# Seven block products instead of eight for a feed-forward layer's gate and up projections, in float32 split into high and low parts

## The chip, the cores and the metric

The kernel runs on one core of a Trainium2 chip. The metric is the device time of one execution in microseconds (us). The core's engines are TensorE (PE, the matrix multiplier; PEld are its weight loads), VectorE (DVE), ScalarE (ACT), GpSimd (POOL) and SyncE (SP, which here only issues DMA transfers). They run their own instruction streams and wait for each other through semaphores. TensorE writes its results to PSUM (8 banks of 128 x 512 float32); everything else lies in SBUF.

## The reference

Two transformer blocks in a row, 1024 tokens of width 1024. Both end in the same kind of feed-forward layer, and the change is to it:

```python
h = rms_norm(h_res, pre_ffn_g[l])                                    # 1024 x 1024
f = silu(einsum('bld,df->blf', h, w_gate[l])) * einsum('bld,df->blf', h, w_up[l])   # d_ff = 2816
f = einsum('blf,fd->bld', f, w_down[l])
h_res = h_res + rms_norm(f, post_ffn_g[l])
```

The second block has the same with `w_ffn_in` (gate and up side by side) and `w_ffn_out`. Before the layer stands the mixer's output projection (`w_out`), a norm and a residual; what the mixers compute (differential attention with a state space model, gating with forgetting attention) plays no part here.

## The kernel before

All matrices are float32. Each operand of a product is split into a high part, rounded to the format that TensorE takes at full rate (float32r), and a low part, the rest. A product is then three matmuls into one PSUM bank, in the helper `three` (L267 to L271): high x high, high x low, low x high.

The input of the layer, transposed (features on partitions), is `xh` and `xl`: 8 feature tiles of 128 x 1024 tokens. D_FF = 2816 makes NF = 22 inner tiles of 128.

Class `Mlp` (L1656) does the layer, for both blocks:

- `pe_in` computes gate (j = 0, banks 0 and 1) or up (j = 1, banks 2 and 3) of one inner tile: 8 feature tiles x 2 token halves x 3 = 48 matmuls of 128x512. `pe_hidden` is both, 96 matmuls.
- ScalarE (`act_hidden`) takes SiLU of the gate from PSUM into `f`, VectorE (`dve_prod`, L1847) multiplies it with up from PSUM, ScalarE makes the high part `mlp_fh` (L1832), VectorE the low part `mlp_fl` (`dve_low`, L1852).
- `pe_down` multiplies a pair of inner tiles with their rows of the down weights: 8 token tiles x 2 column halves x 2 inner tiles x 3 = 96 matmuls, into banks 4, 5 and 6, 7 by turns. VectorE adds each token tile's result to `hbuf` (`dve_add`, L1858, 128x1024), which a memset cleared.
- In the loop of `pe` the order is hidden(f+2), down of the pair before, hidden(f+3); one trip of the loop holds three such pairs (864 matmuls) and there are three trips. Each engine has its own loop.
- The weights come as 512 KB loads on SP's queue into `mlp_raw` (one buffer each for gate, up and down); GpSimd makes both parts (`pool_split`: high L1716, low L1719), each some 128x1024 operation.

Around it: `pe_out` does the output projection. Beside its second half run, tile by tile, `act_beside_out`, `dve_beside_out`, `pool_beside_out` and `sp_beside_out`: square sums (ScalarE, L488), roots (GpSimd, `pool_root1` and `pool_root2`, L500 and L504), norm, residual and scaling (VectorE, L515, L521, L527, the last into `xs_b`), transposition on TensorE (`pe_turn`, L546), high part (ScalarE, L495) and low part (VectorE, L535) of `xh`, `xl`. Before the roots `pool_beside_out` splits the first two weight tiles. `pe_first` is the entry of the layer: it puts the first inner tile's gate and up, by token halves, between the turns of tiles 4 to 7. The last pair of down products (`pe_down_tile` with NP-1) stands alone at the end.

## Time and profile before

| | us |
|---|---|
| runs, median of 3 | 2792.04 (2789.49 to 2795.03) |
| the profiled execution | 2792.63 |
| its span, first to last instruction | 2790.8 |
| TensorE busy in the span | 2565.2 (92%) |
| VectorE, ScalarE, GpSimd busy | 1060.0, 531.4, 915.0 |
| mean granted TensorE clock | 0.958 of full speed |

Busy times of matmuls overlap in the profile, since they are pipelined, so the distance between the starts of matmuls says what one costs. The chain of waits is followed back from the last instruction to what released each; it says which engine's work sets the end. In the lists of single instructions the columns are start, duration, engine, line, operation, output <- inputs, shape and count, and in brackets the engine's idle time before it and who ended it. "issue" is a wait for which the profile shows no other releaser.

### The profile page before, as it was taken

To read this page: it belongs to the slowest core of one execution; us is meant where nothing else is said; L and a number is where in the kernel's file an instruction comes from. 1 tells how busy PE (TensorE), PEld (TensorE's weight loads), DVE (VectorE), ACT (ScalarE), POOL (GpSimd) and SP (SyncE) were. 2 spreads that over 40 slices of the span, in tenths; PEclk is the share of its full clock that TensorE was granted. 3 is DMA by queue.
4 is the path that set the end of the run, shared out by engine and by line. 5 is a ranking of instruction groups with operands and counts; after the bars stand their busy time and mean duration, and the time that the engine had idled before them with its cause. 6 is when DMAs were issued, how large, how long until landed. Compare 5 with 4: busy or idle time off the path is not lost.

```text
span 2790.8 us, 30673 instructions
## 1 busy us (share of the span) xinstructions
PE 2565.2 (92%) x12294; PEld 2073.0 (74%) x12294; DVE 1060.0 (38%) x1624; ACT 531.4 (19%) x1008; POOL 915.0 (33%) x571
## 2 busy tenths in 40 slices
PE   8998777489999999999989998877999999999997
PEld 8977655377788888888878886765778878878885
DVE  5984655436322222222264313663432222222224
ACT  4221344414100000000032002442310000000001
POOL 3210300015433333344374432000553333333332
PEclk8998899689999999999999999996999999999998
DMA  4437300004111111111142112000411111111113
GB/s 134 132 118 195 124 15 1 4 31 159 61 46 46 46 46 46 46 46 46 49 162 64 51 47 91 1 9 16 151 61 46 46 46 46 46 46 46 46 46 128
DMA packets 175980, 180.20 MB, mean 65 GB/s; under 512 B 38344, under 2 KB 138568, under 8 KB 175840
## 3 DMA queue, kind: packets, MB, share of 16 engines
q1 hardware_dynamic: 169968, 163.95, 19.0%
q10 hardware_dynamic: 5872, 14.22, 1.5%
q8 instruction: 107, 1.75, 0.2%
q14 instruction: 33, 0.27, 0.0%
HBM read 147.65 MB, written 30.49 MB: 64 GB/s over the span
## 4 chain that ended last, share of the span: by engine, by line
PE 83%; DVE 6%; ACT 4%; issue 2%; DMA 2%; POOL 2%; SPq 0%; ACTq 0%; POOLq 0%; DVEq 0%
PE ps L269 23%; PE ps L271 23%; PE ps L270 23%; PE ps L1497 3%; PE ps L1527 3%; PE ps L1513 2%; ACT ex L1574 2%; DMA msb<-ssm_lags 1%; DVE hbuf L515 1%; DVE hbuf L521 1%; PE ps L546 1%; DVE hbuf L1858 1%; PE ps L1502 1%; PE ps L2289 1%; PE ps L2242 0%
## 5 line engine op out<-in xcount | busy, mean ns | idle before, releaser
L1847 DVE TENSOR_TENSOR mlp_f<-mlp_f,ps 128x1024 f32<-128x1024 f32 x44 | 53.7, 1221 | 831.6 <-PE ps L271 802.0
L1716 POOL TENSOR_TENSOR mlp_w2h<-mlp_raw,ones 128x1024 fp32r<-128x1024 f32 x44 | 83.4, 1895 | 817.7 <-PE ps L271 732.4
L209 POOL TENSOR_TENSOR wgt<-raw,ones 128x512 fp32r<-128x512 f32 x76 | 86.9, 1143 | 770.5 <-PE ps L271 615.5
L1858 DVE TENSOR_TENSOR hbuf<-hbuf,ps 128x1024 f32<-128x1024 f32 x176 | 214.8, 1220 | 243.6 <-PE ps L271 243.6
L269 PE MATMUL ps<-mlp_w2h,mlp_fh 128*128 128x512 f32 x704 | 280.4, 398 | 11.4 <-issue 7.4
L269 PE MATMUL ps<-xh,mlp_w0h 128*128 128x512 f32 x704 | 278.5, 396 | 7.4 <-ACT mlp_f L1828 5.1
L269 PE MATMUL ps<-xh,mlp_w1h 128*128 128x512 f32 x704 | 278.9, 396 | 2.8 <-DVE xl L535 2.8
L270 PE MATMUL ps<-mlp_w2l,mlp_fh 128*128 128x512 f32 x704 | 279.3, 397 | 0.0
L271 PE MATMUL ps<-mlp_w2h,mlp_fl 128*128 128x512 f32 x704 | 279.3, 397 | 0.0
L270 PE MATMUL ps<-xl,mlp_w1h 128*128 128x512 f32 x704 | 278.7, 396 | 0.0
L271 PE MATMUL ps<-xh,mlp_w1l 128*128 128x512 f32 x704 | 278.7, 396 | 0.0
L271 PE MATMUL ps<-xh,mlp_w0l 128*128 128x512 f32 x704 | 278.0, 395 | 0.0
L270 PE MATMUL ps<-xl,mlp_w0h 128*128 128x512 f32 x704 | 278.0, 395 | 0.0
L1828 ACT ACTIVATE mlp_f<-ps 128x1024 f32<-128x1024 f32 x44 | 45.2, 1027 | 785.6 <-PE ps L271 785.6
L269 PEld LDWEIGHTS ps<-mlp_w2h,mlp_fh 128*128 128x128 f32 x704 | 133.3, 189 | 46.4 <-issue 8.2
L269 PEld LDWEIGHTS ps<-xh,mlp_w0h 128*128 128x128 f32 x704 | 132.3, 188 | 41.1 <-issue 9.5
L269 PEld LDWEIGHTS ps<-xh,mlp_w1h 128*128 128x128 f32 x704 | 132.7, 188 | 35.0 <-DVE xl L535 3.3
L271 PEld LDWEIGHTS ps<-mlp_w2h,mlp_fl 128*128 128x128 f32 x704 | 133.1, 189 | 32.1
L270 PEld LDWEIGHTS ps<-mlp_w2l,mlp_fh 128*128 128x128 f32 x704 | 133.2, 189 | 31.7
L271 PEld LDWEIGHTS ps<-xh,mlp_w1l 128*128 128x128 f32 x704 | 132.7, 188 | 32.0
L270 PEld LDWEIGHTS ps<-xl,mlp_w1h 128*128 128x128 f32 x704 | 132.6, 188 | 31.8
L271 PEld LDWEIGHTS ps<-xh,mlp_w0l 128*128 128x128 f32 x704 | 132.3, 188 | 31.8
(389 smaller groups left out, 4783.0 us busy)
## 6 DMA issues: line engine op xcount, KB each, us to landing
mlp_raw<-in_w_ffn_in SPq DMA_DIRECT2D x44, 512.0 KB, 4.3
h<-hbuf SPq DMA_DIRECT2D x24, 512.0 KB, 2.8
mlp_raw<-in_w_gate SPq DMA_DIRECT2D x22, 512.0 KB, 4.5
mlp_raw<-in_w_up SPq DMA_DIRECT2D x22, 512.0 KB, 4.9
mlp_raw<-in_w_down SPq DMA_DIRECT2D x22, 512.0 KB, 4.6
mlp_raw<-in_w_ffn_out SPq DMA_DIRECT2D x22, 512.0 KB, 4.1
raw<-in_w_in SPq DMA_DIRECT2D x40, 256.0 KB, 2.6
raw<-in_w_out SPq DMA_DIRECT2D x32, 256.0 KB, 2.7
```

The lines of the kernel that those rows point to most:

```text
L209: nc.gpsimd.tensor_tensor(wh[:, s, :], r, ones[:, 0:1].broadcast_to([P, 512]), ALU.mult).then_inc(w_hi, 1)
L269: pe.matmul(out, lhs[0], rhs[0], start=first, stop=False)
L270: pe.matmul(out, lhs[0], rhs[1], start=False, stop=False)
L271: return pe.matmul(out, lhs[1], rhs[0], start=False, stop=last)
L1497: pe.matmul(self.score(item, m, a, b), self.q[rows, t, i * P:(i + 1) * P], self.k[rows, t, a:b], start=True, stop=True)
L1513: t = pe.transpose(ps[0:w, self.tbank(b), j * P:(j + 1) * P], self.ex[:, n % 3, 0, c:c + w], ident[:, :])
L1527: mm = pe.matmul(self.obank(n), self.atb[0:w, b % 3, j, :], self.v[0:w, t, h * self.dv:(h + 1) * self.dv], start=first, stop=last, skip_gr ...
L1574: nc.scalar.activation(self.ex[:, n % 3, m, 0:w], src, ACT.Exp, bias=negmax[:, n % 3, m:m + 1], accum_out=psum_l[:, n % 3, m:m + 1]).then_ ...
L1716: nc.gpsimd.tensor_tensor(self.sh[j][:, b, :], self.raw[:, j, :], ones[:, 0:1].broadcast_to([P, D]), ALU.mult).then_inc(self.s[f"hi{j}"], 1)
L1828: nc.scalar.activation(self.f[:, :], ps[:, 0:2, :].rearrange("p b c -> p (b c)"), ACT.Silu)\
L1847: v.tensor_tensor(self.f[:, :], self.f[:, :], ps[:, 2:4, :].rearrange("p b c -> p (b c)"), ALU.mult).then_inc(self.s["prod"], 1)
L1858: v.tensor_tensor(self.acc[:, i, :], self.acc[:, i, :], ps[:, b:b + 2, :].rearrange("p b c -> p (b c)"), ALU.add)\
```

## The change

Gate and up of one inner tile are seen as one product of a 2 x 2 block matrix (gate and up; low and high half of the 1024 features) with the 2 x 2 blocks of the input (feature halves x token halves). Strassen's algorithm, in the form with 7 products and 15 additions, is used. With gl, gh, ul, uh for the weight blocks (128 x 512) and b11, b21, b12, b22 for those of x:

- weights: s1 = ul + uh, s2 = s1 - gl, s3 = gl - ul, s4 = gh - s2 (GpSimd, `pool_sum`, per inner tile, in float32 before the split)
- input: t1 = b12 - b11, t2 = b22 - t1, t4 = b21 - t2, t3 = b22 - b12, once per layer, built on TensorE by adding matmuls with the identity `posid` or its negative `negid` onto the turned tile in PSUM (`add_block`, `pe_t24`, `pe_t3`: 40 matmuls of 128x512), with high part by ScalarE (`act_t`) and low part by VectorE (`dve_t`); t1 takes the place of b12 in `xh`, `xl`
- products, 12 matmuls each: gl b11, gh b21 (added in bank X), s1 t1 and s4 b22 (bank Z), s2 t2, s3 t3, uh t4 (bank Y, one after the other on top)
- VectorE adds the partial results out of PSUM as they come (u2, u3, p1, half-width 128x512), with SiLU by ScalarE on the two gate halves

The down products are done per inner tile: 48 matmuls, each result added by VectorE, in four pairs of token tiles between the block products; only the last two inner tiles are taken together (96 matmuls). The first result is copied, not added, so the memset goes. ScalarE takes over all high parts (`act_hi`), GpSimd does sums and low parts in half-width operations (low part over the raw weights). The loops have 9 trips of two windows (264 matmuls). The new order of TensorE in a window (one inner tile):

```diff
+        def pe_window(self, pe, f, odd, down=True, begun=False):
+            x = self.BX[odd]
+            early = isinstance(f, int) and f < 2
+            def down_pair(n):
+                if down:
+                    self.pe_down_tile(pe, f - 1, 2 * n)
+                    self.pe_down_tile(pe, f - 1, 2 * n + 1)
+            if not begun:
+                if not early:
+                    self.wait(pe, "prod", f * 2 - 2)
+                self.pe_product(pe, f, odd, "gl", x, True)
+                self.wait(pe, "taken", f * 5 - 1)
+            self.pe_product(pe, f, odd, "s1", self.BZ, True)
+            down_pair(0)
+            if begun:
+                begun()
+            else:
+                self.wait(pe, "taken", f * 5)
+            self.pe_product(pe, f, odd, "s2", self.BY, True)
+            down_pair(1)
+            self.wait(pe, "taken", f * 5 + 1)
+            self.pe_product(pe, f, odd, "s3", self.BY, False)
+            down_pair(2)
+            if not begun:
+                self.pe_x_second(pe, f, odd)      # gh
+            down_pair(3)
+            self.wait(pe, "taken", f * 5 + 3)
+            self.pe_product(pe, f, odd, "s4", self.BZ, False)
+            self.pe_product(pe, f, odd, "uh", self.BY, False)
```

GpSimd, ScalarE and VectorE in the same window (g is the next inner tile, whose weights are prepared):

```diff
+        def pool_window(self, pool, f, odd):
+            g, o = f + 1, 1 - odd
+            self.pool_sum(pool, g, o, "s1", f * 5 + 1)
+            self.pool_lo(pool, g, o, "uh")
+            self.pool_sum(pool, g, o, "s2", f * 5 + 2)
+            self.pool_lo(pool, g, o, "s1")
+            self.pool_sum(pool, g, o, "s3", f * 5 + 3)
+            self.pool_lo(pool, g, o, "gl")
+            self.pool_lo(pool, g, o, "s3")
+            self.pool_sum(pool, g, o, "s4", f * 5 + 4)
+            self.pool_lo(pool, g, o, "s2")
+            self.pool_down_lo(pool, f)
+            self.pool_lo(pool, g, o, "gh")
+            self.pool_lo(pool, g, o, "s4")
...
+        def act_window(self, act, f, odd, middle=None):
...
+                for name in ("uh", "s1", "gl", "s2", "s3"):
+                    self.act_hi(act, g, o, name)
+            self.wait(act, "direct", f * 2 + 2)
+            nc.scalar.activation(x, x, ACT.Silu).then_inc(self.s["x_read"], 1)
...
+                self.act_hi(act, g, o, "gh")
+            self.wait(act, "taken", f * 5 + 4)
+            nc.scalar.activation(self.u2[:, :], self.u2[:, :], ACT.Silu).then_inc(self.s["x_read"], 1)
+            self.act_f_hi(act, f, 1)
...
+                self.act_hi(act, g, o, "s4")
+            self.wait(act, "raw_down", (f + 1) * 16)
+            z = 0 if more else 1
+            nc.scalar.copy(self.d[z][0][:, :], self.d_raw[z][:, :]).then_inc(self.s["f_hi"], 1)
+            self.act_f_hi(act, f, 0)
...
+            adds(4, NT)
+            self.wait(v, "mixed", f * 5 + 4)
+            v.tensor_tensor(u2, u2, z, ALU.add).then_inc(taken, 1)
+            self.wait(v, "x_read", f * 3 + 3)
+            v.tensor_tensor(u3, u2, u3, ALU.mult).then_inc(self.s["prod"], 1)
+            self.wait(v, "mixed", f * 5 + 5)
+            v.tensor_tensor(p1, p1, y, ALU.add).then_inc(taken, 1)
+            self.wait(v, "taken", f * 5 + 5)
+            v.tensor_tensor(p1, p1, x, ALU.mult).then_inc(self.s["prod"], 1)
+            b = 0 if self.last(f) else 1
+            for h, src in ((1, u3), (0, p1)):
+                c = slice(h * HALF, (h + 1) * HALF)
+                self.wait(v, "f_hi", f * 3 + (1 if h else 3))
+                v.tensor_tensor(self.f[b][1][:, c], src, self.f[b][0][:, c].bitcast(F32), ALU.subtract)\
+                    .then_inc(self.s["f_lo"], 1)
```

SP loads the raw down weights of a window once the down tiles of the inner tile before are done, since they lie where the low part lay:

```diff
+            self.wait(sp, "down", f * 8)
+            sp.dma_start(self.d_raw[0][:, :], self.wd[:, bass.ds(f, 1), :].rearrange("p f n -> p (f n)"))\
+                .then_inc(self.s["raw_down"], 16)
```

The entry: turns of tiles 4 to 7 with the additions onto them, and products gl and gh of inner tile 0 between:

```diff
+            turns.pe_turn(pe, 4)
+            out_emptied(pe)
+            turns.x_ready(pe, 3)
+            self.pe_product(pe, 0, 0, "gl", self.BX[0], True)
+            turns.pe_t24(pe, 0)
+            turns.pe_turn(pe, 5)
+            turns.pe_t3(pe, 0)
+            self.pe_x_second(pe, 0, 0)
+            turns.pe_t24(pe, 1)
+            turns.pe_turn(pe, 6)
+            turns.pe_t3(pe, 1)
+            turns.pe_t24(pe, 2)
+            turns.t_ready(pe, 0, 3)
+            turns.pe_turn(pe, 7)
+            turns.pe_t3(pe, 2)
+            turns.pe_t24(pe, 3)
+            turns.t_ready(pe, 2, 3)
...
+            self.pe_window(pe, 0, 0, False, rest)
+            self.pe_window(pe, 1, 1)
+            with pe.Fori(0, 9) as it:
                 for b in range(2):
+                    self.pe_window(pe, it * 2 + (2 + b), b)
+            self.pe_window(pe, NF - 2, 0)
+            self.pe_window(pe, NF - 1, 1, False)
             for i in range(NT):
+                self.pe_down_tile(pe, NF - 2, i, both=True)
```

`pool_beside_out` no longer waits and splits two full weight tiles ahead of the roots: it makes s1 and the low part of uh, and the other blocks of inner tile 0 between the roots, one or two half-width operations at a time. The gains and the scaled tile get buffers of their own for each of the two passes, and the next gains are loaded inside the last window. The weight slots of the output projection and of the second block's projections are dealt in another order.

## Rows read from the trace of the kernel before

**Rows 1.** The page: shares of the chain that ended last.
```profile
PE 83%; DVE 6%; ACT 4%; issue 2%; DMA 2%; POOL 2%; SPq 0%; ACTq 0%; POOLq 0%; DVEq 0%
PE ps L269 23%; PE ps L271 23%; PE ps L270 23%; PE ps L1497 3%; PE ps L1527 3%; PE ps L1513 2%; ACT ex L1574 2%; DMA msb<-ssm_lags 1%; DVE hbuf L515 1%; DVE hbuf L521 1%; PE ps L546 1%; DVE hbuf L1858 1%; PE ps L1502 1%; PE ps L2289 1%; PE ps L2242 0%
```
**Rows 2.** Busy us by stretch: PE, PEld, DVE, ACT, POOL, clock, DMA share, GB/s.
```profile
1260.00:1340.00 80.00, 80.00 (x345) 64.35 (x344) 15.05 (x12) 5.19 (x5) 36.02 (x17) 1.00 0.19 60
```
**Rows 3.** Single matmuls in order of time, first feed-forward layer.
```profile
716.35 0.47 PE L269 MATMUL ps<-xh,mlp_w0h 128*128 128x512 f32 x1 [2.58 <-ACT mlp_f L1828]
...
1141.75 0.40 PE L271 MATMUL ps<-xh,mlp_w1l 128*128 128x512 f32 x1
```
**Rows 4.** Instructions in order of time, entries of both feed-forward layers.
```profile
644.65 0.22 POOL L500 TENSOR_SCALAR tmpa<-stat 128x1 f32<-128x1 f32 x1
...
654.40 1.97 PE L546 MATMUL ps<-ident,xs_b 128*128 128x128 f32 x8 [3.46 <-DVE xs_b L527]
...
682.71 0.40 PE L271 MATMUL ps<-wgt,gyl 128*128 128x512 f32 x1
...
1965.38 1.29 POOL L211 TENSOR_TENSOR wgt<-raw,wgt 128x512 fp32r<-128x512 f32 x1
...
1993.26 1.10 PE L546 MATMUL ps<-ident,xs_b 128*128 128x128 f32 x8 [1.43 <-DVE xs_b L527]
...
2018.90 0.40 PE L271 MATMUL ps<-wgt,mbl 128*128 128x512 f32 x1
...
2050.99 0.47 PE L269 MATMUL ps<-xh,mlp_w0h 128*128 128x512 f32 x1 [2.57 <-ACT mlp_f L1828]
```
**Rows 5.** Single matmuls, start of the last down products, first layer.
```profile
1414.96 0.77 PE L269 MATMUL ps<-mlp_w2h,mlp_fh 128*128 128x512 f32 x1 [3.70 <-issue]
1415.52 0.63 PE L270 MATMUL ps<-mlp_w2l,mlp_fh 128*128 128x512 f32 x1
```
**Rows 6.** Operations on two tiles: duration in ns min/median/max, first and last start.
```profile
L1847 DVE TENSOR_TENSOR mlp_f<-mlp_f,ps x44: 1220/1221/1224, 716.3 to 2747.2; 128x1024 f32<-128x1024 f32 x44
L1852 DVE TENSOR_TENSOR mlp_fl<-mlp_f,mlp_fh x44: 1218/1417/3461, 718.7 to 2749.5; 128x1024 fp32r<-128x1024 f32 x44
L1719 POOL TENSOR_TENSOR mlp_w0l<-mlp_raw,mlp_w0h x44: 2396/2407/3271, 637.8 to 2680.8; 128x1024 fp32r<-128x1024 f32 x44
```
**Rows 7.** Instructions in order of time, behind products of TensorE.
```profile
783.62 0.40 PE L269 MATMUL ps<-xh,mlp_w0h 128*128 128x512 f32 x1
783.82 1.22 DVE L1858 TENSOR_TENSOR hbuf<-hbuf,ps 128x1024 f32<-128x1024 f32 x1 [1.58 <-PE ps L271]
783.86 1.90 POOL L1716 TENSOR_TENSOR mlp_w2h<-mlp_raw,ones 128x1024 fp32r<-128x1024 f32 x1 [40.35 <-PE ps L271]
...
828.61 1.22 DVE L1847 TENSOR_TENSOR mlp_f<-mlp_f,ps 128x1024 f32<-128x1024 f32 x1 [18.28 <-PE ps L271]
829.87 1.05 ACT L1832 CAST mlp_fh<-mlp_f 128x1024 fp32r<-128x1024 f32 x1 [11.43 <-DVE mlp_f L1847]
```
**Rows 8.** Groups of instructions of half width: busy us, mean ns, idle before.
```profile
L535 DVE TENSOR_TENSOR xl<-ps,xh 128x512 fp32r<-128x512 f32 x48 | 30.8, 682 | 18.9 <-ACT xh L495 18.9
L495 ACT CAST xh<-ps 128x512 fp32r<-128x512 f32 x48 | 25.5, 584 | 33.0 <-PE ps L546 33.0
```
**Rows 9.** The weight loads: a wait of GpSimd, and landing times.
```profile
791.85 1.90 POOL L1716 TENSOR_TENSOR mlp_w2h<-mlp_raw,ones 128x1024 fp32r<-128x1024 f32 x1 [3.61 <-DMA mlp_raw<-in_w_down]
...
DMA to landing us min/median/max: 3.4/4.6/8.8
```
**Rows 10.** Single matmuls behind the four returns of TensorE's loops.
```profile
940.40 0.40 PE L269 MATMUL ps<-xh,mlp_w0h 128*128 128x512 f32 x1
...
1142.30 0.49 PE L269 MATMUL ps<-xh,mlp_w0h 128*128 128x512 f32 x1
...
2275.18 0.49 PE L269 MATMUL ps<-xh,mlp_w0h 128*128 128x512 f32 x1 [0.89 <-issue]
...
2478.28 0.50 PE L269 MATMUL ps<-xh,mlp_w0h 128*128 128x512 f32 x1 [1.26 <-issue]
```

More of the change, by code:

```diff
@@ L1891, in _program, with dve @@
+        def dve(self, v):
+            self.dve_window(v, 0, 0, False)
+            v.wait_ge(sem("stored"), 16 * NT * (1 + 2 * self.turn))
+            self.dve_window(v, 1, 1)
+            with v.Fori(0, 9) as it:
+                for b in range(2):
+                    self.dve_window(v, it * 2 + (2 + b), b)
+            self.dve_window(v, NF - 2, 0)
+            self.dve_window(v, NF - 1, 1, False)
+            self.wait(v, "f_lo", 2 * NF)
     o1 = at("o1", [P, NT, HALF], F32, O_X)
```

570 lines of the change are left out of this document (327 added, 243 removed).

## Prediction

> **What bounds the kernel now.** I read the page's totals and its chain of waits first, then the table of stages, then the feed-forward stages by groups, then single instructions where something waits. Both feed-forward blocks together take about half of the span, and TensorE is on 83% of the chain that ended last, and 69% of the span lies in the three lines of the helper `three` [rows 1]. In the middle of a feed-forward block TensorE is busy for 80.00 of 80 us at granted clock 1.00, while VectorE works 15 us of the 80 and GpSimd 36 [rows 2]. So a matmul less there is time less, as long as nobody new has to be waited for. The price of one: matmul 1 of `pe_hidden(1)` starts at 716.35, matmul 1824 (96 + 2 x 864) at 1141.75; that is 0.2333 us each, gate, up and down alike [rows 3]. Outside this steady part there are two places where TensorE waits: the entry (it waits for the first tile's `xs_b`, for the tiles' turns, and for SiLU's first result) and the end (3.70 us before the last down products, and then some matmuls that last 0.63 instead of 0.40 us, at the lower of the two clocks) [rows 4, 5].
>
> **What is removed.** Inner tiles 1 to 21 of each block take 7 x 12 = 84 gate/up matmuls instead of 96: 21 x 12 = 252 fewer. The down matmuls are as many as before (20 x 48 + 96 = 1056). 2 x 252 x 0.2333 = **-117.6 us**. The 8 more VectorE additions per pair of tiles (1.22 us each [rows 6]), and the smaller splits on GpSimd and ScalarE are in the shade of a window of 132 matmuls = 30.8 us: VectorE 8 x 1.22 + 9 x 0.68 = 15.9, GpSimd 11 x 1.3 + 2.4 = 16.7, ScalarE some 9 us. The memset that goes (one per block) was not on TensorE's path. SP issues five loads per inner tile (four of 256 KB, one of 512) for three of 512 KB; the bytes are the same, and each waits only for a product of the window before the one that needs it, down excepted (below). Neither engine becomes the bound by its sum; what matters is the order inside a window.
>
> **The one tight chain in a window.** Let 0 be the end of product s4 (so uh runs 0 to 2.8, the next window's gl to 5.6, s1 to 8.4, and at 8.4 down pair 0 wants this tile's `f` and `down` parts). A consumer starts 0.20 (VectorE) or 0.24 us (GpSimd) after the start of TensorE's next matmul, and ScalarE 0.04 us after VectorE's end (828.61 + 1.22 to 829.87) [rows 7]. Half-width operations (128x512) take 0.68 on VectorE, 0.59 on ScalarE [rows 8], 1.29 on GpSimd [rows 4]. At 0.20 VectorE adds z to u2 (to 0.9), ScalarE does SiLU (to 1.6), VectorE wants the product u3 at 1.6 to 1.7. GpSimd makes sum s4 from 0.24 to 1.53 and begins `lo s2` at 1.60. The product has both inputs in SBUF. Such a VectorE operation is what gets long when GpSimd works: `mlp_fl` (both inputs SBUF) takes 1.22 to 3.46 us, `mlp_f` (one input PSUM) 1.220 to 1.224 always, and GpSimd's 2.41 becomes 3.27 in turn [rows 6]. One waits for the whole instruction of the other. If GpSimd is first: product 2.9 to 3.5; ScalarE: f high half 2 to 4.1, high part of s4 to 4.7, high part of down (1.05) to 5.7, f half 1 to 6.2. The raw down weights are there by then: after `down` is done (-2.6), today's next load of the same 512 KB keeps GpSimd waiting for 3.61 us in all [rows 9], so about 1.0. GpSimd's low part of down runs 5.75 to 8.15; VectorE's low part of f half 1, ready at 6.3, must wait until 8.15 and ends at 8.8. TensorE begins pair 0 at 8.9 instead of 8.4, everything behind it in its queue (s2, s3, gh, s4, uh) moves with it, and with a slow first matmul, as behind other stops (0.1), that is **0.6 us in each of the windows 1 to 20: 40 x 0.6 = +24 us**. If VectorE is first at 1.6, everything is 1.1 us earlier and pair 0 has no wait. The two differ by 0.1 us in the order at 1.6, which I cannot settle from rows; I take GpSimd first, since its 1.60 needs two steps and VectorE's 1.65 needs three handovers. Bounds: 0 and 1.0 per window (eight handovers, each up to 0.05 longer than I took it), 0 to 40 us.
>
> The Trainium skill ("SBUF — State Buffer", Terms) says of the port pair that VectorE and GpSimd share that it is locked for the full instruction and that the loser fully blocks. The rows of `mlp_fl` agree (3.46 less 1.22 is nearly one GpSimd operation of 2.41). Without that rule, with shared bandwidth, the chain would be short enough for no stop.
>
> **The entry.** Today from the last out-projection matmul's end to `pe_hidden(1)`: (last start 682.71 or 2018.90, plus 0.23) 682.94 to 716.35 = 33.4 us, and 2019.13 to 2050.99 = 31.9 [rows 3, 4]. After: inner tile 0's products and 40 more matmuls (9.3 us) that build t2, t4, t3, each tile of them needing a ScalarE copy and a VectorE subtraction, in order, behind the turn. I walked it: turn 4 and its additions 0.9 to 2.2, gl to 5.0, wait for `lo` of tile 4 (6.4), pe_t24(0) to 8.0, turn 5 to 9.2. ScalarE: casts for tile 5 (2 x 0.53), square (1.2), keep, t2 to 12.4; VectorE to 13.1. Then t3(0), gh, pe_t24(1), turn 6 to 20.5. Each later tile repeats turn 1.3 + casts 1.1 + three T copies 1.6 + subtraction 0.7 + t3 0.5 + t24 1.4, about 6.5 us: turn 7 ends 26.8, s1 starts 32.1 and ends 34.9. Window 0 has no down pairs to cover VectorE: wait for t3's last tile 2.0, s2 2.8, wait 1.1, s3 2.8, wait 1.6, s4 and uh 5.6: 50.8. One stretch of lower clock after an idle of 4 us, as after the 3.70 us one [rows 5] (8 matmuls, each some 0.2 longer): 52.4. So 19.0 and 20.5 us longer than now. Against it: GpSimd no longer splits two full weight tiles (2 x (1.90 + 2.41) = 8.6 us [rows 6, 9]) ahead of the first root, which starts at 644.65 [rows 4], but does a half-width sum and a low part (2.6), with ScalarE's first square then the later of the two, so the first `xs_b` is some 5 us earlier; the waits of 3.46 us (with the lower clock behind it some 2.0 more, as in [rows 5]) and 1.43 us before `pe_turn(0)` go [rows 4]: -5.5 and -1.6. Entries together **+32.4 us**. Its bounds: +17, if the walk's 39.5 us are only 0.6 of that because the copies of T overlap better than in my order; +45, if TensorE's clock is low for most of the entry.
>
> **The end.** In window 21 there are no down pairs, so s3 waits 1.1 us for VectorE. Then the f parts lie over fz, so ScalarE does f half 2 (0.59) and the down part (1.05) only after uh, GpSimd 2.4: 4.4 us instead of 3.7. **+3.6 us** for both.
>
> **The loops.** TensorE returns to a loop's head 2 times per block now: 0.0, 0.4, 1.2, 1.5 us beyond the pitch (mean 0.8) [rows 3, 10]. After: 8 returns per block. They come between uh and gl, so they lie inside the 0.6 us stop where that exists: 16 x 0.25 - 3.1 = **+1 us**; without that stop 16 x 0.6 - 3.1 = +6.5. The Trainium skill ("Runtime: NRT & Kernel Launch", Instruction fetch mechanics) says that a taken branch outside the resident window forces a fetch before execution goes on, and gives 2048 instructions for TensorE. The present body (1728 matmul and load instructions plus waits) would hardly fit, the new one (528 plus waits) would, and then all returns would be free; the row with 0.0 shows that size alone does not force a stop.
>
> **Sum** against the profiled execution (2792.6 us, span 2790.8; its median of runs is 2792.0, so the same): 2792.6 - 117.6 + 24 + 32.4 + 3.6 + 1 = **2736 us**.
>
> **Rivals.**
> A (forecast, 0.5): GpSimd wins the port at s4's end; 2736.
> B (0.25): VectorE wins, no stop at pair 0: 2792.6 - 117.6 + 32.4 + 3.6 + 6.5 = 2717.5. For it: VectorE's three operations could hand over in 0.03 us each, as some do [rows 7].
> C (0.12): each return costs the 1.5 us of the longest row, on top of the stop: 2736 - 1 + 16 x 1.5 - 3.1 = 2756. Against it: the other returns are cheaper.
> D (0.06), slower: the raw down weights land late. They can be asked for only when down tile 7 is done, 11 us before they are needed as parts. At the longest landing of this kernel's weight loads, 8.8 us [rows 9], ScalarE starts its part at 6.3, GpSimd ends at 9.8, VectorE at 10.5, and pair 0 stops 2.2 us: 40 x 2.25 = 90, 2801 us. It decides from 2.0 us a window (81 / 40). Against it: the median is 4.6, and today the next load follows alone in its queue, as here.
> The rest (0.07) is other faster outcomes. A stop of 0.6 us does not cost the clock: after an idle time of 1.26 us [rows 10] and even 2.57 us [rows 4] the next matmul took 0.50 and 0.47 us, not 0.77 as behind the 3.70 us [rows 5].
>
> **Numbers.** Predicted 2736; range 2708 to 2772 (B and its entry a little better; C and a worse entry). About 0.2% is what a measurement of this kernel tells from no change. Faster 0.92 (A, B, C and the rest), same 0.02, slower 0.06 (D).
>
> **What would show it.** TensorE instructions lower by 2 x (252 + 12 - 40) = 448 matmuls. Pair 0's first matmul with an idle time of about 0.5 us put down to VectorE's low part of f (A) or none (B); the product u3 lasting 1.9 us rather than 0.7 (A). From the out-projection's end to the start of window 1 about 52 us. GpSimd's first root some 4 us earlier against the out-projection. The prediction is wrong if the pitch is not 0.233, if idle stands before a product other than those named, or if the T part takes much more or less than 20 us over today's.

## The result and the profile after

The changed kernel took 2704.61 us (median of 4 runs, 2693.33 to 2706.45), the kernel before 2790.76 beside it: ratio 0.9682, 95% interval 0.9652 to 0.9711, so 3.2% faster. The forecast was 2736 with a range from 2708 to 2772. The side was right; the time lies 31 us below the forecast and 3 us below the range. The profiled execution of after, 2693.33 us with a span of 2691.2, is the fastest of its four. The account by stages below compares spans (2790.8 before, a difference of 99.6 us); a second set of runs of the unaltered kernel gave 2697.65 us (2696.16 to 2704.77) and a span of 2694.6.

The shares of the chain that ended last, from the page of after, and the table of stages of after over the same 80 us as in [rows 2]:

```profile
PE 80%; DVE 7%; ACT 5%; issue 3%; DMA 2%; POOL 2%; SPq 0%; ACTq 0%; POOLq 0%; DVEq 0%
PE ps L267 22%; PE ps L268 22%; PE ps L269 22%; PE ps L1546 3%; PE ps L1576 3%; PE ps L1562 2%; ACT ex L1623 2%; DVE hbuf L513 1%; PE ps L562 1%; DMA msb<-ssm_lags 1%; DVE hbuf L2045 1%; PE ps L1551 1%; PE ps L2528 1%; PE ps L2480 1%; PE ps L436 1%
```
```profile
1260.00:1340.00 80.00, 80.00 (x349) 65.27 (x348) 46.65 (x46) 20.19 (x34) 44.51 (x31) 1.00 0.16 49
```

TensorE is busy for all of the 80 us at granted clock 1.00, as before, but with 349 matmuls instead of 345. So each is shorter, which the forecast had no term for. VectorE went from 15.05 to 46.65 us and GpSimd from 36.02 to 44.51; neither is the bound.

Single matmuls of after in order of time, first layer: the start of windows 1 and 21.

```profile
731.49 0.40 PE L267 MATMUL ps<-xh,mlp_glh 128*128 128x512 f32 x1
...
1339.36 0.40 PE L267 MATMUL ps<-xh,mlp_glh 128*128 128x512 f32 x1
```

(1339.36 - 731.49) / 20 = 30.39 us a window, 0.2302 us a matmul, against 0.2333 in [rows 3] and 30.8 us a window in the forecast. No window in between is longer, so there is no stop in them and no gap at the loop's returns.

The entry of the first layer, matmuls in order of time; the last out-projection matmul is the row at 679.17:

```profile
651.95 1.10 PE L544 MATMUL ps<-ident,xs_a 128*128 128x128 f32 x8 [0.94 <-DVE xs_a L525]
...
679.17 0.40 PE L269 MATMUL ps<-wgt,gyl 128*128 128x512 f32 x1
...
685.95 0.50 PE L562 MATMUL ps<-xh,negid 128*128 128x512 f32 x1 [1.81 <-DVE xl L533]
...
692.42 0.79 PE L562 MATMUL ps<-xh,negid 128*128 128x512 f32 x1 [3.46 <-DVE t2l L600]
...
702.87 0.80 PE L562 MATMUL ps<-xh,negid 128*128 128x512 f32 x1 [2.76 <-DVE t2l L600]
...
717.45 0.50 PE L267 MATMUL ps<-t2h,mlp_s2h 128*128 128x512 f32 x1 [1.40 <-DVE t3l L600]
...
721.27 0.50 PE L267 MATMUL ps<-t3h,mlp_s3h 128*128 128x512 f32 x1 [0.78 <-DVE mlp_u L2063]
...
725.82 0.50 PE L267 MATMUL ps<-xh,mlp_s4h 128*128 128x512 f32 x1 [1.50 <-DVE mlp_u L2068]
```

From 679.17 + 0.23 to 731.49 are 52.1 us (forecast 52.4; 33.4 before by [rows 3, 4]). In the second layer, 1967.93 + 0.23 to 2018.26, they are 50.1 (31.9 before). The waits stand where the forecast's walk had them: for the low part of the last split tile, for each tile's T copies, and in window 0 before s2, s3 and s4. The lower clock (matmuls of 0.63 us) came twice in the first entry, behind the waits of 3.46 and 2.76 us, where the walk had it once.

The end, in answer to [rows 5]:

```profile
1365.15 0.76 PE L267 MATMUL ps<-mlp_dh,mlp_fh 128*128 128x512 f32 x1 [5.12 <-POOL mlp_dzl L1846]
1365.71 0.63 PE L268 MATMUL ps<-mlp_dl,mlp_fh 128*128 128x512 f32 x1
```

5.12 us of idle time (4.89 in the second layer) instead of 3.70, and the same 0.63 us matmuls behind it.

The place on which the forecast turned, s4's end, in the middle of the first layer of after: instructions of VectorE, GpSimd and ScalarE in order of time, then pair 0's first matmul, which shows no idle time.

```profile
880.87 0.69 DVE L2071 TENSOR_TENSOR mlp_u<-mlp_u,ps 128x512 f32<-128x512 f32 x1 [1.50 <-PE ps L269]
880.91 1.30 POOL L1833 TENSOR_TENSOR mlp_s_raw<-mlp_gh_raw,mlp_s_raw 128x512 f32<-128x512 f32 x1 [7.08 <-PE ps L269]
881.59 0.63 ACT L2016 ACTIVATE mlp_u<-mlp_u 128x512 f32<-128x512 f32 x1 [2.83 <-DVE mlp_u L2071]
882.25 0.69 DVE L2073 TENSOR_TENSOR mlp_u<-mlp_u,mlp_u 128x512 f32<-128x512 f32 x1 [0.70 <-ACT mlp_u L2016]
882.29 1.81 POOL L1840 TENSOR_TENSOR mlp_s2l<-mlp_s_raw,mlp_s2h 128x512 fp32r<-128x512 f32 x1
...
885.22 2.71 POOL L1846 TENSOR_TENSOR mlp_dl<-mlp_d_raw,mlp_dh 128x1024 fp32r<-128x1024 f32 x1 [1.12 <-ACT mlp_dh L2022]
885.75 2.73 DVE L2082 TENSOR_TENSOR mlp_fl<-mlp_p,mlp_fh 128x512 fp32r<-128x512 f32 x1
...
889.01 0.39 PE L267 MATMUL ps<-mlp_dh,mlp_fh 128*128 128x512 f32 x1
```

The product u3 starts at 882.25 and GpSimd's low part of s2 at 882.29. VectorE is 0.04 us ahead, it takes its 0.69, and GpSimd takes 1.81 instead of 1.3. In each of the 42 windows where the two meet VectorE is ahead, by 0.03 to 0.10 us. At 885.75 it is the other way round: VectorE's second low part of f lasts 2.73 us, as long as GpSimd's low part of down, and ends at 888.48, 0.5 us before it is needed. The groups over all windows of after say the same (columns: busy us, mean ns of one, idle time before):

```profile
L1840 POOL TENSOR_TENSOR mlp_s2l<-mlp_s_raw,mlp_s2h 128x512 fp32r<-128x512 f32 x44 | 78.7, 1788 | 3.7
L2073 DVE TENSOR_TENSOR mlp_u<-mlp_u,mlp_u 128x512 f32<-128x512 f32 x44 | 30.7, 697 | 30.7 <-ACT mlp_u L2016 30.7
L2082 DVE TENSOR_TENSOR mlp_fl<-mlp_p,mlp_fh 128x512 fp32r<-128x512 f32 x42 | 114.4, 2724 | 3.6
```

**Where the 99.6 us are.** From window 1 to the first of the last down products: 698.61 us before (716.35 to 1414.96) and 633.66 after (731.49 to 1365.15) in the first layer, 699.85 (2050.99 to 2750.84) and 633.42 (2018.26 to 2651.68) in the second: -131.4 together. The entries: +18.7 and +18.2. The rest, in which the earlier roots lie: -5.1. The forecast for the three was -89.0 (-117.6 + 24 + 1 + 3.6), +39.5 and -7.1. So nearly all of the miss is in the windows and the end: 42.4 us.

### The profile page after: what moved, and what is told of

It is laid out like the page before. It is cut to its first block, busy times and chain, and to the rows that moved or that the text cites. A ratio compares the mean times of both kernels' runs of the same rounds, so it can differ in the third digit from the quotient of the medians.

```text
span 2691.2 us, 33052 instructions
## 1 busy us (share of the span) xinstructions
PE 2446.8 (91%) x11846; PEld 1984.9 (74%) x11846; DVE 1493.4 (55%) x2116; ACT 797.6 (30%) x1512; POOL 1117.1 (42%) x835
## 4 chain that ended last, share of the span: by engine, by line
PE 80%; DVE 7%; ACT 5%; issue 3%; DMA 2%; POOL 2%; SPq 0%; ACTq 0%; POOLq 0%; DVEq 0%
PE ps L267 22%; PE ps L268 22%; PE ps L269 22%; PE ps L1546 3%; PE ps L1576 3%; PE ps L1562 2%; ACT ex L1623 2%; DVE hbuf L513 1%; PE ps L562 1%; DMA msb<-ssm_lags 1%; DVE hbuf L2045 1%; PE ps L1551 1%; PE ps L2528 1%; PE ps L2480 1%; PE ps L436 1%
## 5 line engine op out<-in xcount | busy, mean ns | idle before, releaser
L2045 DVE TENSOR_TENSOR hbuf<-hbuf,ps 128x1024 f32<-128x1024 f32 x320 | 390.6, 1221 | 252.4 <-PE ps L269 232.0
L267 PE MATMUL ps<-mlp_dh,mlp_fh 128*128 128x512 f32 x672 | 264.4, 393 | 12.8 <-POOL mlp_dzl L1846 10.0
L269 PE MATMUL ps<-mlp_dh,mlp_fl 128*128 128x512 f32 x672 | 263.1, 392 | 0.0
L268 PE MATMUL ps<-mlp_dl,mlp_fh 128*128 128x512 f32 x672 | 262.5, 391 | 0.0
L267 PEld LDWEIGHTS ps<-mlp_dh,mlp_fh 128*128 128x128 f32 x672 | 126.6, 188 | 43.7 <-POOL mlp_dzl L1846 10.8
L268 PEld LDWEIGHTS ps<-mlp_dl,mlp_fh 128*128 128x128 f32 x672 | 126.7, 189 | 27.5
L269 PEld LDWEIGHTS ps<-mlp_dh,mlp_fl 128*128 128x128 f32 x672 | 126.4, 188 | 27.7
L1846 POOL TENSOR_TENSOR mlp_dl<-mlp_d_raw,mlp_dh 128x1024 fp32r<-128x1024 f32 x42 | 113.8, 2710 | 46.5 <-ACT mlp_dh L2022 46.5
L2082 DVE TENSOR_TENSOR mlp_fl<-mlp_p,mlp_fh 128x512 fp32r<-128x512 f32 x42 | 114.4, 2724 | 3.6
L1562 PE MATMUL ps<-ident,ex 128*128 128x128 f32 (+1 forms) x464 | 80.7, 285 | 18.7 <-ACT ex L1623 15.9
L267 PE MATMUL ps<-x1h,chunk_w 128*128 128x352 f32 (+2 forms) x256 | 89.5, 350 | 2.5 <-DVE x1l L713 1.6
L269 PE MATMUL ps<-x1h,chunk_w 128*128 128x352 f32 (+2 forms) x256 | 87.9, 343 | 0.0
```

The source lines that it names most:

```text
L267: pe.matmul(out, lhs[0], rhs[0], start=first, stop=False, skip_group_check=over)
L268: pe.matmul(out, lhs[0], rhs[1], start=False, stop=False, skip_group_check=over)
L269: return pe.matmul(out, lhs[1], rhs[0], start=False, stop=last, skip_group_check=over)
L1562: t = pe.transpose(ps[0:w, self.tbank(b), j * P:(j + 1) * P], self.ex[:, n % 3, 0, c:c + w], ident[:, :])
L1846: nc.gpsimd.tensor_tensor(self.d[z][1][:, :], self.d_raw[z][:, :], self.d[z][0][:, :].bitcast(F32), ALU.subtract).then_inc(self.s["split"], 1)
L2045: v.tensor_tensor(self.acc[:, i, :], self.acc[:, i, :], src, ALU.add).then_inc(self.s["added"], 1)
```

## The experiments

Two things were to be explained: no stop at pair 0, and matmuls that are shorter than 0.2333 us, but not all. In window 6 of after the products start like this:

```profile
883.46 0.40 PE L267 MATMUL ps<-xh,mlp_glh 128*128 128x512 f32 x1
886.25 0.40 PE L267 MATMUL ps<-xh,mlp_s1h 128*128 128x512 f32 x1
...
908.34 0.39 PE L267 MATMUL ps<-xh,mlp_s4h 128*128 128x512 f32 x1
911.06 0.40 PE L267 MATMUL ps<-t4h,mlp_uh0h 128*128 128x512 f32 x1
913.85 0.40 PE L267 MATMUL ps<-xh,mlp_glh 128*128 128x512 f32 x1
```

12 matmuls of gl take 2.79 us (0.2328 each), of s4 2.72 (0.2267), of uh 2.79. The means over windows 2 to 20: gl 2.797, s1 2.758, s2, s3 and uh 2.792, gh 2.796, s4 2.720, and 2.737 for 12 down matmuls. The granted clock is 1.00 for all.

**e0_same.** The changed kernel again, unaltered.

> The changed kernel once more, unaltered, to get a second profiled execution: the first one took 2693.3 us, the other three 2704.5 to 2706.5. Theory 1 (the order at s4's end differs from execution to execution): a slower execution shows the product u3 at 1.9 us in some windows and a stop of some 0.3 us before pair 0 there. Theory 2 (the distance between matmuls differs): all windows look alike, u3 takes 0.69 us, but a window is longer than 30.40 us; 11 us over 44 windows are 0.25 us a window. Theory 3: the 11 us lie outside the two feed-forward layers.

Measured 2697.65 us (2696.16 to 2704.77), ratio 0.9676 [0.9648, 0.9705]. Window 30.393 us, the same to three digits. What differs between profiles lies outside: window 1 starts at 728.71 instead of 731.49. Over the profiles of all kernels that are equal up to there the first gl starts between 675.1 and 685.1 us. So some 10 us of every time here is this scatter, and single effects are read from the window below.

**e1_unrolled.** TensorE's loop written out.

```diff
-            with pe.Fori(0, 9) as it:
+            for it in range(9):
```

> TensorE's loop of 9 trips is written out, so it never returns and all its instructions come as one stream. Theory R (the short loop body is why the matmuls stand closer in s4 and in the down pairs, 0.227 us instead of 0.233, since its instructions don't have to be fetched again): windows go back to 132 x 0.2333 = 30.8 us, plus 40 x 0.4 = 16 us. Theory P (the distance depends on where the operands lie): windows stay at 30.4 us, time the same within 0.2%.

Measured 2693.54 us (2691.16 to 2697.3), ratio 0.9658 [0.9632, 0.9684]; window 30.393, every product as in after. Whether the instructions come as a loop or as one stream doesn't set the pitch (the distance from one matmul's start to the next), and the eight returns a layer of a body of 264 matmuls had cost nothing.

**e2_port_lost.** ScalarE takes the high part of s4 ahead of SiLU of u2, so that the product comes later than GpSimd's low part of s2.

```diff
+            if more:
+                self.act_hi(act, g, o, "s4")
             nc.scalar.activation(self.u2[:, :], self.u2[:, :], ACT.Silu).then_inc(self.s["x_read"], 1)
             self.act_f_hi(act, f, 1)
-            if more:
-                self.act_hi(act, g, o, "s4")
```

> ScalarE makes the high part of s4 before the SiLU of u2 instead of behind it, so VectorE's product u3 comes 1.2 us later and finds GpSimd in the low part of s2. My forecast's term: product 1.9 us or so until its end, everything behind it later, and pair 0 stops 0.4 to 0.6 us in 40 windows: +16 to +24 us. If the chain to pair 0 has more room than I took: no stop, same time.

Measured 2705.72 us (2702.83 to 2707.76), ratio 0.9697 [0.9671, 0.9723]. Windows of 30.62 and 30.52 us in the two layers: 20 x (0.23 + 0.13) = 7 us, and the time is 8 us above e0's. GpSimd is first (its low part of s2 takes 1.30), the product starts 2.56 us after the start of u2's addition instead of 1.38, and still pair 0 loses only 0.2 us. This edit had taken one of ScalarE's four operations out of the chain behind the product (the high part of s4, some 0.5 us). So it wasn't the forecast's case in full, and a cleaner one was needed (e4).

**e3_homes_swapped.** The weight tiles of gl and s4 exchanged in SBUF.

```diff
-            one = {"gl": block("gl", O_WH), "gh": block("gh", O_WH + 4096), "s3": block("s3", tail),
-                   "s4": block("s4", tail + 4096), "s1": block("s1", tail + 24576), "s2": block("s2", tail + 28672)}
+            one = {"gl": block("gl", tail + 4096), "gh": block("gh", O_WH + 4096), "s3": block("s3", tail),
+                   "s4": block("s4", O_WH), "s1": block("s1", tail + 24576), "s2": block("s2", tail + 28672)}
```

> The weight blocks gl and s4 change homes: gl goes from the low address range (the old weight slots) to the high one behind hbuf, s4 the other way. Nothing else changes. Theory P (matmuls whose two operands both lie above the x tiles' start stand 0.227 us apart, those with one operand in the old weight slots 0.233): gl becomes fast (and s1 from its first matmul), s4 slow; the total within 0.2%. Theory Q (it depends on the PSUM bank, s4 being in bank 2 and gl in 0 or 3): s4 stays at 0.227 and gl at 0.233.

Measured 2700.22 us (2689.6 to 2700.57), ratio 0.9665 [0.9634, 0.9697]; window 30.38 and 30.35. gl now takes 2.724 us and s4 2.796; s1, right behind gl, went from 2.758 to 2.72. The pitch goes with the place of the tile and not with the order of the products or their PSUM bank. That both operands must lie in the upper part of SBUF fits this run.

**e4_port_late.** SiLU of u2 in two instructions, so that its result is a little later. In the rows below the product starts 1.48 us after u2's addition instead of 1.38, and GpSimd's low part 1.43 instead of 1.42.

```diff
-            nc.scalar.activation(self.u2[:, :], self.u2[:, :], ACT.Silu).then_inc(self.s["x_read"], 1)
+            nc.scalar.activation(self.u2[:, 0:P], self.u2[:, 0:P], ACT.Silu)
+            nc.scalar.activation(self.u2[:, P:HALF], self.u2[:, P:HALF], ACT.Silu).then_inc(self.s["x_read"], 1)
```

> The changed kernel with SiLU of u2 in two instructions (128 and 384 columns), so that its result comes some 0.2 us later; nothing else. In the changed kernel VectorE's product u3 beat GpSimd's low part of s2 to the port by 0.04 us. Theory 1 (the one that asks first has the port for its whole instruction, and the forecast's chain was right in all but who is first): GpSimd's low part of s2 takes 1.30 instead of 1.81 us, the product u3 starts some 1.1 us later, VectorE's second low part of f ends at about 8.8 us after s4's end, and pair 0 stops 0.5 to 0.6 us in each of windows 1 to 20: a window of 30.9 to 31.0 instead of 30.39, the kernel 20 to 24 us longer. Rival 2 (the chain has slack that the forecast did not see, as in the run where the high part of s4 went ahead and a window took 30.57): 30.5 to 30.6, 5 to 9 us. Rival 3 (VectorE has the port whoever asks first): the product lasts 0.69 or up to 1.9 us, GpSimd's operation is long, a window is 30.4, and the time is that of the changed kernel.

Measured 2723.7 us (2719.33 to 2729.6), ratio 0.9756 [0.9736, 0.9775]: 26 us more than e0. Windows of 31.03 and 30.94 us. Instructions of this kernel in order of time:

```profile
888.21 1.29 POOL L1840 TENSOR_TENSOR mlp_s2l<-mlp_s_raw,mlp_s2h 128x512 fp32r<-128x512 f32 x1
888.26 1.78 DVE L2074 TENSOR_TENSOR mlp_u<-mlp_u,mlp_u 128x512 f32<-128x512 f32 x1 [0.79 <-ACT mlp_u L2017]
...
892.33 2.40 POOL L1846 TENSOR_TENSOR mlp_dl<-mlp_d_raw,mlp_dh 128x1024 fp32r<-128x1024 f32 x1 [2.84 <-ACT mlp_dh L2023]
892.80 2.47 DVE L2083 TENSOR_TENSOR mlp_fl<-mlp_p,mlp_fh 128x512 fp32r<-128x512 f32 x1 [0.83 <-ACT mlp_fh L1989]
...
895.52 0.49 PE L267 MATMUL ps<-mlp_dh,mlp_fh 128*128 128x512 f32 x1 [0.43 <-DVE mlp_fl L2083]
```

Now GpSimd is 0.05 us ahead and takes 1.29, the product 1.78 instead of 0.69, and pair 0 idles 0.43 us behind VectorE's low part of f; with its slow first matmul a window is on average 0.64 us longer (0.55 in the second layer). That is the forecast's case, with its price (0.6 us, 24 in all). Counted from s4's end (the start of uh, 886.58), GpSimd's low part of down runs from 5.75 to 8.15 us, VectorE's low part of f ends at 8.69 and pair 0 starts at 8.94; the forecast had 5.75 to 8.15, 8.8 and 8.9.

This run also holds its own control. GpSimd is first in 36 of the 42 windows where the two meet; in the first two and the last one of each layer they start within 0.01 us of each other, VectorE has its 0.69, and the window behind the first two lasts 30.39 us as in e0, with the same split SiLU:

```profile
764.52 0.69 DVE L2074 TENSOR_TENSOR mlp_u<-mlp_u,mlp_u 128x512 f32<-128x512 f32 x1 [0.79 <-ACT mlp_u L2017]
764.52 1.84 POOL L1840 TENSOR_TENSOR mlp_s2l<-mlp_s_raw,mlp_s2h 128x512 fp32r<-128x512 f32 x1
```

Windows 3 to 19, all behind a lost race, last 31.09 to 31.14 us in the first layer and 30.99 to 31.02 in the second. So the lost race costs the time, and the split of SiLU by itself nothing: 26 us of this kernel hang on which of two engines asks first, and 0.10 us of delay turned it.

**e5_homes.** This tests "both operands in the upper part" by exchanging gl with s3, and gh with s2.

```diff
-            one = {"gl": block("gl", O_WH), "gh": block("gh", O_WH + 4096), "s3": block("s3", tail),
-                   "s4": block("s4", tail + 4096), "s1": block("s1", tail + 24576), "s2": block("s2", tail + 28672)}
+            one = {"s3": block("s3", O_WH), "s2": block("s2", O_WH + 4096), "gl": block("gl", tail),
+                   "s4": block("s4", tail + 4096), "s1": block("s1", tail + 24576), "gh": block("gh", tail + 28672)}
```

> The changed kernel with the weight tiles of gl and s3 exchanged in SBUF, and those of gh and s2; all instructions and their order as before. Theory P (a matmul takes 0.2267 us where both its operands lie in the upper part of SBUF, from the x tiles on, and 0.2333 where one of them lies below): s2 and s3 read t2 and t3, which lie below, and stay at 2.79 us wherever their weights are; gl and gh go from 2.80 to 2.72 and s1 behind gl from 2.76 to 2.72; a window is 30.2 instead of 30.39, the kernel 7 to 8 us shorter. Rival (the length goes with the order of the products or with their PSUM bank, and the exchange of gl and s4 in the run before only happened to fit): nothing changes, 30.39.

Measured 2685.12 us (2679.48 to 2695.45), ratio 0.9627 [0.9602, 0.9651]; windows of 30.08 and 30.05. gl 2.735 and gh 2.720 as expected; but s2 and s3, whose two operands now both lie in the lower part, went to 2.730 too. The theory falls in this form; "both on the same side" would fit.

**e6_homes_end.** As e5, and at the end of a layer TensorE begins with inner tile 20's parts for two feature tiles, which need nothing of tile 21.

```diff
+            self.wait(pe, "split", self.split_of(NF - 1, "down"))
+            self.wait(pe, "f_lo", (NF - 1) * 2)
+            for z in range(2):
+                if z:
+                    self.wait(pe, "split", 8 * NF + 1)
+                    self.wait(pe, "f_lo", 2 * NF)
+                for i in range(2):
+                    self.pe_down_part(pe, i, z)
+                    if z:
+                        after_tile(pe, i)
-            for i in range(NT):
+            for i in range(2, NT):
```

> As the run with the exchanged tiles, and the last down products of a block begun with inner tile 20's parts for feature tiles 0 and 1 (12 matmuls, 2.8 us), which need nothing of the last inner tile; only then does TensorE wait for tile 21's parts. If the 4.9 to 5.1 us of waiting at the end of a block are waiting for tile 21's parts alone: the wait gets 2.7 us shorter in each block, together 5 to 6 us below the run with exchanged tiles alone, and perhaps the slow first matmuls behind it go as well. Rival (the 12 matmuls run into a wait of their own, or the lower clock falls on the rest): no difference, or under 2 us.

Measured 2683.95 us (2679.26 to 2685.1), ratio 0.9609 [0.9593, 0.9626]. The times can't tell it from e5. In the traces the wait went from 5.19 and 4.89 to 2.55 and 2.23 us, and from the start of window 21 to the tile behind the last down products (the matmul of `ident,xs_b` that waits for `xl`, in the first layer) it is 52.1 us instead of 55.9 (1337.05 to 1389.16; 1333.93 to 1389.85). The 12 matmuls at 0.63 us that stand behind the wait in e5's first layer are gone too. Later adds of VectorE take back a part (waits of 2.02 and 1.17 us, where e5 has 0.87, 0.61 and 0.74). In the second layer, from the start of window 21 to the end of the span, it is 62.6 us instead of 64.9. Together these are the 6 us expected, less than the scatter of the times.

**e7_long_body and e9_long_again.** TensorE's loop as 3 rounds of 6 windows, run once and then again several times.

```diff
-            with pe.Fori(0, 9) as it:
-                for b in range(2):
-                    self.pe_window(pe, it * 2 + (2 + b), b)
+            with pe.Fori(0, 3) as it:
+                for b in range(6):
+                    self.pe_window(pe, it * 6 + (2 + b), b % 2)
```

> The changed kernel with TensorE's loop made of 3 rounds of 6 windows instead of 9 rounds of 2: a body of 1584 matmul and load instructions, about as many as the kernel before has in its loop (1728). Theory (a return costs when the body is too long to be held, and nothing when it is short): at some of the 2 returns of each block TensorE's next matmul starts 0.4 to 1.5 us beyond the pitch, as in the kernel before. Rival (the returns of the kernel before cost for another reason, such as what stood behind the loop's head): none of the returns shows a gap, as none of the 8 does now.

> The kernel with TensorE's loop of 3 rounds of 6 windows once more, now timed: its two returns in the first layer cost 4.8 and some 6 us with the lower clock behind them, its two in the second nothing. Theory (a body too long to be held is fetched again at a return, and whether it arrives in time varies): again some of the four returns cost 1 to 6 us, not all need be the same ones, and the median lies 3 to 12 us above that of the changed kernel. Rival (the gaps of the one profile were a disturbance): no gap at a return, the time of the changed kernel.

Measured 2708.08 us (one run), then 2710.54 (2708.96 to 2718.12), ratio 0.9717 [0.9691, 0.9744], 13 us above e0. Matmuls at the first return of e7:

```profile
945.59 0.49 PE L267 MATMUL ps<-xh,mlp_glh 128*128 128x512 f32 x1
948.82 0.40 PE L268 MATMUL ps<-xl,mlp_glh 128*128 128x512 f32 x1 [2.74 <-issue]
...
949.63 0.63 PE L268 MATMUL ps<-xl,mlp_glh 128*128 128x512 f32 x1
```

In both profiles each of the two returns of the first layer costs about 5 us (4.7 to 5.6): 2.7 to 3.0 us of idle time behind gl's first matmul, and then matmuls of 0.63 at the lower clock. Windows 2 to 20 of that layer hold 10 of the 13 us. The two of the second layer cost nothing. With 2-window bodies none of the 16 returns shows a gap. So what a return costs depends on the length of the body (1584 matmul and load instructions here, 1728 in the kernel before, 528 in the changed one); why the second layer is spared stays open. The Trainium skill ("Runtime: NRT & Kernel Launch", Instruction fetch mechanics) gives TensorE an instruction memory of 2048 instructions and says that a taken branch to a target outside the current window forces a fetch. Here returns did cost at about 1600 matmul and load instructions plus waits, below that number, though in one layer of two, and were free at a third of that.

**e8_uh_low.** As e6, with the tile uh0 exchanged with p1 and the raw ul, so that both operands of uh lie in the lower part in every second window.

```diff
-            self.block = [dict(one, uh=block("uh0", tail + 32768)), dict(one, uh=block("uh1", tail + 40960))]
-            self.ul = at(f"{tag}_ul", [P, 4, P], F32, 5376)
-            self.p1 = at(f"{tag}_p1", [P, HALF], F32, 3328)
+            self.block = [dict(one, uh=block("uh0", 3328)), dict(one, uh=block("uh1", tail + 40960))]
+            self.ul = at(f"{tag}_ul", [P, 4, P], F32, tail + 34816)
+            self.p1 = at(f"{tag}_p1", [P, HALF], F32, tail + 32768)
```

> As the run with the exchanged tiles and the new end, and the weight tile uh0 (even inner tiles) exchanged with p1 and the raw ul, so that it lies in the lower part of SBUF as its moving operand t4 does; uh1 (odd inner tiles) stays in the upper part. The theory formed from the last call (0.2333 us where one operand lies below the x tiles and the other not, 0.227 where both lie on the same side): uh takes 2.73 instead of 2.79 us in even windows and 2.79 still in odd ones, a mean window is 30.02 to 30.05 instead of 30.05 to 30.08; 1.3 us in all, less than the times can show. Rival (uh is slow because of its place in the order or its PSUM bank): 2.79 in all.

Measured 2679.23 us (2669.43 to 2687.01), ratio 0.9596 [0.9571, 0.9621]. uh0 still takes 2.792 us, like uh1. "Same side" falls as well. Set beside each other, the differences of the two operands' addresses give a rule that fits all products so far: the weight slots and the T tiles start at O_WH = 7808 plus multiples of 4096, x at 65536, the upper tiles at x plus multiples of 1024, uh0 in this run at 3328. Fast pairs differ by 0 modulo 256 bytes (an upper tile with x; s2, s3 at O_WH with t2, t3; f with d), slow pairs by 128 (gl, gh with x; s2, s3, uh in the upper part with T; uh0 at 3328 with t4). In the kernel before every weight stands at 128 from its other operand.

**e10_aligned, e11_before_aligned, e12_quarter, e13_best.** The start of the lower part moved: 128 bytes in the changed kernel, 128 in the kernel before, 64 in the changed one, and 128 together with e6's end.

```diff
-O_WH = 7808
+O_WH = 7936
```

(e12 has 7872 instead.)

> The changed kernel with the start of the lower part of SBUF (weight slots, gl, gh, t2, t3, t4, last tile's parts) 128 bytes higher, nothing else. Theory M: a matmul of these takes 0.2267 us where the addresses of its two operands differ by a multiple of 256 bytes, and 0.233 where they differ by 128 more than one. It fits all products of the runs so far (fast: s1, s4 and down, 1024 or 4096 times a whole number apart; gl or s4 on the tiles' other side; s2 and s3 in the lower part with t2 and t3; slow: gl, gh, s2, s3, uh as they are, and uh0 at 3328 with t4), which the rule by upper and lower part does not. Then all of a window's 132 matmuls go at 0.2267: 29.9 to 30.0 us instead of 30.39, 19 us less in the two layers, and some 12 us less in the other projections, whose weights lie in the same slots: 28 to 33 us in all. Rival 1 (512 bytes or more must divide the difference): window 30.39 as before or longer. Rival 2 (upper and lower part): no change.

Measured 2669.88 us (2668.6 to 2673.79), ratio 0.9571 [0.9557, 0.9586], 28 us below e0; the windows give 19 of them, the rest lies outside them. Window 29.94 and 29.92; every product takes 2.72 us:

```profile
910.89 0.39 PE L267 MATMUL ps<-t4h,mlp_uh0h 128*128 128x512 f32 x1
913.61 0.39 PE L267 MATMUL ps<-xh,mlp_glh 128*128 128x512 f32 x1
916.33 0.39 PE L267 MATMUL ps<-xh,mlp_s1h 128*128 128x512 f32 x1
```

> The kernel before with the same 128 bytes. Theory M: all its gate, up and down products have weights in the moved slots and their other operand outside, so all of them go from 0.2333 to 0.2267: 6336 x 0.0066 = 42 us in the two layers and some 12 us in the other projections, 2791 to about 2737 us. Then the change is worth about 70 us on top of it (0.974) rather than the 88 it was measured at (0.968), as 17 us of that were the addresses of its new tiles. Rivals 1 and 2: no change.

Measured 2748.53 us (2740.72 to 2752.12) beside 2788.45 for the kernel before: ratio 0.9843 [0.9823, 0.9864]. 6 matmuls of it in the first layer, 1.36 us or 0.227 each, where [rows 3] has 0.2333:

```profile
1127.67 0.39 PE L269 MATMUL ps<-xh,mlp_w1h 128*128 128x512 f32 x1
...
1129.03 0.39 PE L269 MATMUL ps<-xh,mlp_w1h 128*128 128x512 f32 x1
```

In the profiles the two layers give 38 us (from the first gate matmul to the last down matmul 758.0 and 756.7 us before, 737.9 and 738.7 here) and the stretch between them 6 (578.2 to 572.6). The pitch of the other projections fell too: of `wgt` with `xh` from 0.232 to 0.227 us. By their counts that is some 10 us in the seven groups whose pitch fell, an estimate from pitch times number; about half of it shows in the span.

> The changed kernel with the lower part only 64 bytes higher, so that its tiles stand at 64 bytes from a multiple of 256 from the others. Theory M says nothing of 64 bytes: if the part of a 256-byte line that is read twice sets the price, the slow products stay slow (2.79) or come between (2.75), and s1, s4 and down, whose operands both lie above, stay at 2.72. A window is 30.3 to 30.4. If the rule is by 128 bytes, all are slow or fast alike.

Measured 2700.7 us (one run), window 30.33: gl 2.80, s2 and s3 2.80, uh 2.80, gh 2.75, s1 2.74, s4 2.72. At 64 bytes most are as slow as at 128, gh comes between; what both have in common with the fast ones (an upper tile with x) stays fast.

> The changed kernel with the 128 bytes and the new end (inner tile 20's parts for two feature tiles ahead of the wait). By the runs before: the 28 to 33 us of theory M and the 6 us of the end, about 2664 us, ratio 0.954. If theory M falls: 2693 us.

Measured 2663.01 us (2659.72 to 2673.9), ratio 0.9552 [0.953, 0.9575]: the fastest of all, 4.5% below the kernel before, as expected within 1 us.

## Why the prediction was wrong

**Removed matmuls, -117.6.** The count was right. The page gives 11846 TensorE matmuls for 12294, 448 fewer. The price of 0.2333 holds for the removed ones, since in the kernel before all gate, up and down matmuls have it.

**The step that failed: "I take GpSimd first".** The term of +24 us was put in for a race that the rows left open by 0.1 us. It went the other way, by 0.03 to 0.10 us, in each of the 42 windows (VectorE's product took at most 0.85 us in all 44): rival B. The chain behind it was right in its order and its price, as e4 shows, where the race is lost: a product of 1.78 us (forecast 1.9), a stop of 0.43 us plus a slow first matmul, 0.55 to 0.64 us a window (forecast 0.6), 26 us in all (24). The reason given for the choice was "its 1.60 needs two steps and VectorE's 1.65 needs three handovers". The forecast's own numbers don't give 1.65: with 0.04 us for each handover they are 0.20 + 0.68 + 0.04 + 0.59 + 0.04 = 1.55, ahead of GpSimd's 1.60, and the rest is rounding up at two steps (to 0.9 and to 1.6). In the rows above, counted from s4's end (uh's first matmul, 880.66), VectorE began at 1.59 and GpSimd at 1.63: SiLU took 0.63 instead of 0.59, the handovers to and from ScalarE 0.03 each, GpSimd's 0.08. So the sum had the winner right before it was rounded, though by a margin hardly larger than the errors of its steps. The second instruction ends a little under its own time behind the first: in after 884.10 - 882.94 = 1.16 us for a low part that takes 1.29 alone, in e4 890.04 - 889.50 = 0.54 for a product that takes 0.69. By the Trainium skill's rule ("SBUF — State Buffer", Terms: the pair is locked for the full instruction and the loser fully blocks) it would be the whole of its time; these two rows agree but for some 0.14 us.

**A second term that failed: the pitch.** The forecast took 0.2333 us for matmuls the change leaves or adds, because in the kernel before "gate, up and down alike" have it. But they were alike for one reason: all their weights lay at 128 bytes modulo 256 from the other operand. The change puts s1, s4 and the down parts at 0. For the 2724 matmuls of windows 1 to 21 (20 x 132 + 84) that is 2724 x (0.2333 - 0.2302) = 8.4 us a layer, 17 in all. It is a gift of the memory map and not of the algorithm: e10 and e11 take it out, and then the change is worth 2748.53 - 2669.88 = 79 us (ratio 0.971) instead of 86. In the stretches from window 1 to the last down products, which scatter less, the change gives 112.9 us with both kernels aligned (1360.7 to 1247.8) for 131.4 as they were: 18.5 less. The trace of before had the hint in the product of the forget gate (`xh` with `wfh`, `wfl`), whose weights lie in the upper part: behind its first ten matmuls it ran at 0.227 (six matmuls from 1504.29 to 1505.65).

**Loops, +1 (or +6.5 without a stop).** The returns cost nothing, so the term was -3.1, what the kernel before had paid. The forecast carried its 0.25 to 0.6 us a return over from a body three times as long, though it named the rule by which a short body is free and gave it no chance of its own. e7 and e9 show that the length counts: with three times the windows in the body, and the returns at the same place between uh and gl, some of them cost again.

**Entries, +32.4.** 52.1 and 50.1 us against 52.4 forecast for each: +18.7 and +18.2 for +19.0 and +20.5. The earlier root took the waits before `pe_turn(0)` from 3.46 to 0.94 and from 1.43 to none, but later turns now wait too (0.49 and 0.32 us in the first layer, 0.55 in the second); the stretches outside give -5.1 for -7.1. This is right within the scatter, though not in every step: the walk had one stretch of the lower clock, and the first entry had two.

**The end, +3.6.** The stop became 5.12 and 4.89 instead of 4.4, and s3's wait 0.78 instead of 1.1 in each layer: 2 x (5.0 + 0.78 - 3.7) = +4.2.

**The sum** for the windows and the end: -89.0 forecast, less 24 for the stop, less 17 for the pitch, less 4.1 for the loops (+1 to -3.1), plus 0.6 for the end: -133.5, where -131.4 was measured. The scatter of the rest moves the median by several us: the profile lies 11 us below its own median. So it is partly luck that the median lies only 3 us outside the range: against the profiled execution it would be 15.

**What stays open.** Why 64 bytes make some products slow and gh less so, why a slow product is still felt in the first 8 matmuls of the one behind it (s1 in after: 2.758), and why long bodies return for free in the second layer. In e5 s2 and s3 stay at 2.730 instead of 2.720, as only their first and last matmul are longer (0.231 and 0.233); there the addresses of both operands move by 128 against those of the products beside them, which no run here tests alone.

## What to carry to other kernels

A race closer than the handover times can't be called from rows: give both outcomes their price, don't round the steps on the way, and after the change see which of the two waited, since 0.10 us there can cost a good part of the gain (26 of 86 us here). Before a matmul's pitch is carried over to tiles at new addresses, compare the addresses of the two operands modulo 256 bytes (what is left of each after division by 256); one constant, moved by 128 bytes, gave 40 us of 2788 in the kernel before and 28 in the changed one. Where a time scatters by 10 us in stages that the edit doesn't touch, a period measured in the trace (one window here, 30.393 us in three runs) decides what the medians can't.
